# Latent attention of a decoder layer: the next head's projections moved behind this head's scores, its squares behind the exponential

## The reference

```python
q = split_heads(rms_norm(c_q, mla_cq_norm) @ mla_w_uq, MLA_HEADS)       # 256 -> 96 per head
kv = split_heads(rms_norm(c_kv, mla_ckv_norm) @ mla_w_ukv, MLA_HEADS)   # 128 -> 64 + 64 per head
k_nope, v = jnp.split(kv, [MLA_NOPE_DIM], axis=-1)
k = jnp.concatenate([k_nope, k_rope_h], axis=-1)                        # k_rope_h: shared, 32
q, k = rms_norm(q, mla_q_norm), rms_norm(k, mla_k_norm)                 # over the 96
# rope on the last 32 of q and k, then causal softmax attention, scale 96 ** -0.5
o_mla = merge_heads(block_causal_attention(q, k, v)) @ w_branch_mla
g_fox, g_mla = jnp.split(jax.nn.sigmoid(gate_logit + b_gate), 2, axis=-1)
```

## Time and profile before

| | |
|---|---|
| median of 3 runs | 2617.26 us (2610.24 to 2620.54) |
| the profiled execution | 2618.03 us |
| its span | 2616.2 us |
| TensorE busy | 2435.0 us (93%) |
| VectorE busy | 1423.7 us (54%) |
| ScalarE busy | 967.5 us (37%) |
| GpSimd busy | 507.2 us (19%) |
| latent attention | about 1190 to 1757 us from the span's start |

### The profile page before, as it was taken

How to read it: one execution, slowest core, us unless ns; L and a number is a source line. 1 busy time by engine, 2 the same in 40 slices (tenths; PEclk the granted TensorE clock), 3 DMA queues, 4 the chain that set the end, 5 groups by cost and what they waited for, 6 DMA issues and landing times. The chain is left out here.

```text
span 2616.2 us, 37156 instructions
## 1 busy us (share of the span) xinstructions
PE 2435.0 (93%) x14204; PEld 2155.9 (82%) x14204; DVE 1423.7 (54%) x2052; ACT 967.5 (37%) x1619; POOL 507.2 (19%) x634
## 2 busy tenths in 40 slices
PE   6999999999959999977998999989998999999999
PEld 6899999999958887876777777778876888887887
DVE  7665555555456557533444444445367666555553
ACT  5332333333245444432333333335234333333332
POOL 0023200000033244321222222232320323000000
PEclk8999999999979999989999998889998999999999
DMA  4365632565230000011111110014432676336653
GB/s 182 124 211 188 216 110 100 224 222 182 85 129 1 26 25 1 1 33 43 36 36 34 34 35 28 28 47 151 169 137 82 201 230 216 119 103 242 221 194 112
DMA packets 132699, 298.00 MB, mean 114 GB/s; under 512 B 10096, under 2 KB 57072, under 8 KB 129216
## 3 DMA queue, kind: packets, MB, share of 16 engines
q1 hardware_dynamic: 132544, 295.88, 32.7%
HBM read 206.99 MB, written 88.72 MB: 113 GB/s over the span
## 5 line engine op out<-in xcount | busy, mean ns | idle before, releaser
L1070 DVE TENSOR_TENSOR f_w_lo<-f_rw,f_w_hi 128x1024 fp32r<-128x1024 f32 x154 | 196.2, 1274 | 221.4 <-ACT f_w_hi L590 221.4
L833 PE MATMUL f_ps<-u_hi,f_w_hi 128*128 128x260 f32 (+1 forms) x1056 | 284.0, 323 | 25.9 <-DVE f_w_lo L1070 13.2
L833 PE MATMUL f_ps<-u_lo,f_w_hi 128*128 128x260 f32 (+1 forms) x1056 | 283.0, 323 | 0.0
L833 PE MATMUL f_ps<-u_hi,f_w_lo 128*128 128x260 f32 (+1 forms) x1056 | 282.6, 322 | 0.0
L590 ACT CAST f_w_hi<-f_rw 128x1024 fp32r<-128x1024 f32 x154 | 161.2, 1047 | 164.6 <-PE f_ps L833 157.4
L833 PE MATMUL f_ps<-f_far_hi,f_w_hi 128*128 128x260 f32 (+1 forms) x792 | 211.9, 322 | 8.7 <-DVE f_ev L1086 8.7
L833 PEld LDWEIGHTS f_ps<-u_hi,f_w_hi 128*128 128x128 f32 x1056 | 178.3, 192 | 42.3 <-DVE f_w_lo L1070 14.6
L833 PE MATMUL f_ps<-f_far_lo,f_w_hi 128*128 128x260 f32 (+1 forms) x792 | 210.9, 321 | 0.0
L833 PE MATMUL f_ps<-f_far_hi,f_w_lo 128*128 128x260 f32 (+1 forms) x792 | 210.7, 320 | 0.0
L833 PEld LDWEIGHTS f_ps<-u_hi,f_w_lo 128*128 128x128 f32 x1056 | 177.9, 192 | 14.2
L833 PEld LDWEIGHTS f_ps<-u_lo,f_w_hi 128*128 128x128 f32 x1056 | 177.7, 191 | 14.2
(11 more groups left out here) (394 smaller groups left out, 6128.5 us busy)
## 6 DMA issues: line engine op xcount, KB each, us to landing
f_rw<-in_gu SPq DMA_DIRECT2D x88, 512.0 KB, 4.4
f_rw<-kept_dsum SPq DMA_DIRECT2D x32, 704.0 KB, 5.1
f_rw<-kept_hid SPq DMA_DIRECT2D x33, 520.0 KB, 5.6
f_rw<-in_down SPq DMA_DIRECT2D x24, 704.0 KB, 4.2
f_rw<-kept_hid SPq DMA_DIRECT2D x33, 512.0 KB, 5.5
h_in<-in_wd SPq DMA_DIRECT2D x11, 1024.0 KB, 7.0
kept_dsum<-h_in SPq DMA_DIRECT2D x44, 256.0 KB, 3.0
h_out<-in_wd SPq DMA_DIRECT2D x11, 1024.0 KB, 7.3
```

Source lines behind the costliest of these rows:

```text
L833: last = nc.tensor.matmul(out[:, b, 0:N], w[:, c], u[:, b * N:(b + 1) * N], start=(j < 3 and k == 0 and i == 0), stop=(k == 3 and i == 2), ...
L1070: nc.vector.tensor_tensor(slot(w_lo, st), src, slot(w_hi, st).bitcast(F32), ALU.subtract).then_inc(wlo_done, 1)
```

## The change

It changes the order on two engines. On TensorE, `products` of the next head moves from the head of the block to the place behind `scores`; in the first head's own preparation it moves behind the first maxima and gates of the block. On ScalarE, the square is taken out of `early` and made a function of its own, which is called behind `exponential` (and, in the first head's preparation, behind `copy_logits`).

```diff
@@ ScalarE: early, square @@
                     nc.scalar.copy(split_of(h, u)[0][0:DK, t0:t0 + n], x32[0:DK, u % 2, 0:n]).then_inc(xhi_done, 1)
+
+            def square(p, h, w):
                 if w < NU:
                     is_q, c = units[w]
                     t0, n = QK_TOKENS[c]
@@ ScalarE: head @@
                     exponential(p, h, w)
                     if more:
+                        square(p, h + 1, w)
                         late(p, h + 1, w)
                         gate_weights(p, h + 1, w, more=next_gate)
@@ ScalarE: first head's preparation @@
             for w in range(NW):
                 early(0, 0, w)
                 copy_logits(0, 0, w)
+                square(0, 0, w)
                 late(0, 0, w)
                 gate_weights(0, 0, w)
@@ TensorE: head @@
                 for w in range(NW):
-                    if more and w < NU:
-                        products(p, h + 1, w)
                     if more:
                         maxima(p, h + 1, w, 0)
                         gates(p, h + 1, w, 0)
                     scores(p, h, w)
+                    if more and w < NU:
+                        products(p, h + 1, w)
                     if more:
                         maxima(p, h + 1, w, 1)
                         gates(p, h + 1, w, 1)
@@ TensorE: first head's preparation @@
             for w in range(NW):
+                maxima(0, 0, w, 0)
+                gates(0, 0, w, 0)
                 if w < NU:
                     products(0, 0, w)
-                maxima(0, 0, w, 0)
-                gates(0, 0, w, 0)
                 maxima(0, 0, w, 1)
                 gates(0, 0, w, 1)
                 prepare(0, 0, w)
```

## The result

The change makes the kernel faster: 2556.43 us (median of 4 runs, 2553.94 to 2561.75) against 2617.18 us (4 runs, 2610.24 to 2620.54), a ratio of 0.9774 with a 95% interval of 0.9749 to 0.9799. The forecast was 2559. The profiled execution took 2556.62 us, its span is 2554.8.

The account below looks back on a forecast made before the run. TensorE was taken as the bound, losing time to projection waits and the lower clock; 33.8 - 1.4 - 0.7 + 27 = 58.7 us, and 2618.0 - 58.7 - 0.8 = 2559 us, range 2543 to 2588.

Parts of the forecast that it names:

- Projections: In blocks 2 to 5 of seven heads, gates and scores cover the scaling: waits 47.8 to 14 us, 33.8 back.
- Squares: In block 0 of seven heads, the sums wait 0.1 us for the later square: +0.7 us.
- Row of maxima: In block 0, the last score product waits 0.2 us for the DMA, seven times: +1.4 us.
- First head's preparation: Before the seven heads, gains and costs of the new order sum to 0, between -3 and +3 us.
- Clock: In the seven heads, low-level running behind the projection waits mostly goes: 27 us back, bounds 0 and 34.
- The rival that the dips stay: Sparse sums, broadcasts and small scores cause the low clock; 31.7 us come back, 2586 us; chance 0.17.
- The ring: Exponential, square, sums, inverse root, GpSimd's iteration and remainder form a loop lengthening all 42 blocks: 2634 us; chance 0.02.
- the wait for the squares: TensorE's wait moves to the sums, half a microsecond each; 21 of 31.7 us go, 2607 us; chance 0.03.
- a wait that slips along: VectorE's scaling slips by as much as the projection, so it waits as before: 2617 us; chance 0.03.

Follow-up runs that it names:

- b: The changed kernel with the projections back at the head of the block, squares still behind the exponential: 2629.34 us, ratio to before 1.0046.
- c: The changed kernel with the projections behind one gate group but ahead of the scores: 2570.46 us, ratio 0.9824.
- h: The changed kernel with d's edit, and the finish of the head before one block earlier (FINISH_1 2 to 1): 2545.98 us, ratio 0.9737.
- f: The changed kernel with the first head's preparation in its old order: 2554.81 us in one execution.
- g2: The changed kernel with long TensorE waits, for GpSimd's remainder of the same block, added in blocks 7 to 12: 2686.63 us in one execution.
- g3: The changed kernel with one wait a head, for GpSimd's remainder of the same block, in block 10: 2570.77 us in one execution.
- g1: The changed kernel with short TensorE waits, for the exponential of the same block, added in blocks 7 to 12: 2592.22 us in one execution.
- a: The changed kernel with the square back ahead of the logit copy and the exponential in the seven heads: 2566.36 us, ratio 0.9802.
- d: The changed kernel with the k scaling reading the bank first and k projections waiting only for that: 2547.80 us, ratio 0.9756.

## Why the prediction was right

**The bound and the place.** TensorE was the bound, and the projections' waits were the loss: b brings them back and with them the whole time. Of the 60.7 us by which the seven heads shortened the sum gave 58.7. The forecast for the total, 2559, is 2.6 us above the median. That it comes so near is in part luck: what lies outside the seven heads adds up to 0.7 us between the two profiled spans (5.8 - 1.6 - 4.9), and of its parts only the preparation's place was in the sum. The 4.9 in particular is the dip in the last head of the traced execution of before.

**Projections.** Predicted: 14 us of waits stay, 33.8 come back. Measured at the weight loads: 15.3 stay, 32.5 come back. In TensorE's own idle time 42.5 us (25.2 + 17.3) have become 8.9, so 33.6 come back:
```profile
PE mla_bank L2438 <- DVE mla_x L2627: 7.7, 14, 0.8
PE mla_bank L2435 <- DVE mla_x L2614: 1.2, 7, 0.2
```
The forecast by block was 0.21, 0.85, 0.33 and 0.58 us; the timeline shows 0.24, 0.85, 0.25 and 0.83 at the loads. Two of them, from one head of the kernel after (block 3's with what follows it):
```profile
1321.17 0.94 PEld L2435 LDWEIGHTS mla_bank<-cq,mla_w_head 128*128 128x128 f32 x4 [0.24 <-DVE mla_x L2614]
...
1326.70 0.59 ACT L2385 ACTIVATE mla_rden<-mla_bank 64x512 f32<-64x512 f32 x1
...
1327.33 0.63 ACT L2387 ACTIVATE mla_rden<-mla_rden 64x512 f32<-64x512 f32 x1
...
1327.97 0.19 PEld L2438 LDWEIGHTS mla_bank<-ckv,mla_w_head 128*64 128x64 f32 x2 [0.85 <-DVE mla_x L2627]
...
1328.39 0.59 ACT L2373 COPY mla_logit<-mla_bank 128x512 f32<-128x512 f32 x1
1329.02 0.19 PEld L73 LDWEIGHTS mla_bank<-u_hi,mla_gate_hi 128*128 128x128 f32 x1 [0.86 <-ACT mla_logit L2373]
```
Block 5, whose scores I priced at 0.70 without a row of their own, is off at the loads alone: TensorE's idle time there is 0.40 us, which is the 1.80 of before less the cover of 1.41, and in block 3 it is 0.70 against 1.80 - 1.14 = 0.66. The cover counts by its length, the gate group's (c) and the scores'.

**The copy of the logits** was the term left out. Its row grew by 4.1 us, but most of that passes while the projection still streams: in block 3 the next gate product starts 0.96 to 1.08 us behind the start of the k projection in six of the seven heads, against 0.79 in the seventh, before and in h, and that adds up to 1.5 us. The same rows show where it comes from: in block 3 ScalarE finishes the head before (lines 2385 and 2387) from 1326.70 to 1327.96, then makes x_hi, and only then copies the logits; TensorE, which used to spend that time waiting for the scaling, now comes to the next gate product sooner, and its load waits 0.86 us there (the product, at 1329.02, has 0.20 us of idle TensorE before it). The prediction named this copy in the first head's preparation and not in the seven heads. What was late next should have been asked of ScalarE too; h confirms the place.

**Squares**: 0.7 us predicted, 0.3 measured. **Row of maxima**: 1.4 predicted, 2.1 measured (7 waits, 0.4 at most). **First head's preparation**: 0 predicted within 3, -1.6 measured, and by f -1.8. Block 0 of the same head, for the first two of these:
```profile
1311.74 0.19 PEld L2530 LDWEIGHTS mla_bank<-mla_q_hi,mla_k_hi 98*128 98x128 f32 x1 [0.23 <-DMA mla_q_hi<-mla_m_lo]
1312.08 1.45 PE L2435 MATMUL mla_bank<-cq,mla_w_head 128*128 128x384 f32 x4
...
1313.57 0.49 ACT L2334 ACTIVATE mla_sq<-mla_bank 96x384 f32<-96x384 f32 x1 [0.70 <-PE mla_bank L2435]
1314.36 0.77 PE L2461 MATMUL mla_bank<-ones,mla_sq 96*128 96x1 f32 x6
```
The last score product waits 0.23 us for the rows (0.2 was worked out), and the square ends 2.0 us after the projection's start, 0.3 before the sums begin.

**Clock.** I took 27 of 34 us; all of the 64.8 low microseconds went, and TensorE was busy in 63.8 of them, which is 63.8 / 2 = 31.9 us. The terms of the sum then read: 33.6 + 31.9 - 1.5 - 2.1 - 0.3 = 61.6, 0.9 more than the 60.7; the row of maxima and the squares are taken from the loads, and so at their upper bound. With the rows of the loads throughout it would be 32.5 + 32.4 - 4.1 - 2.1 - 0.3 = 58.4. TensorE's "issue" waits of line 73, which fell from 16.2 to 9.6 us, are in neither.

What did not hold is the reason given for this term: that a wait lowers the clock only behind a broadcast and a row of one-column sums. g2 and g3 show the low level behind waits between dense products. What counts there is first the length of TensorE's idle time. In g2, 26 of the 28 idle times of 1.6 to 2.7 us were followed by a low stretch, and 3 of the 14 of 1.0 to 1.4; in g3, four of seven of 1.7. Before the change, 16 low stretches stood behind the 28 waits: behind 10 of the 14 with 1.8 to 1.9 us of idle TensorE and behind 6 of the 14 with 1.2 to 1.3. With at most 1.2 (c) or 0.8 us (g1 and the change) there is none in the seven heads. The idle time need not be one piece: in a, in one head of seven, the low stretch follows an idle 1.04 us that came behind another of 0.70, 1.9 us from the end of one to the end of the other.

But the part about the neighbours isn't refuted whole. Idle times of 1.22 us behind broadcast and sums were followed by the low level in 5 of 12 cases before the change, and those of 1.07 to 1.19 us behind a gate group in none of 14 in c. No run has the same length in both places, so what the gate group does beside shortening the wait stays open. The change does both, and its waits are well below either; so the price came out right though the reason isn't whole.

The rival that the dips stay, 17 in 100, fell: none is left in the seven heads. The Trainium skill (TensorE: Matmul & The Clock Gate, "Why this matters for your kernels") warns only of idle gaps longer than the 1.7 us of g3; here the trace disagrees, since shorter ones lower the clock too, and the measurement decides. The ring, the wait for the squares and a wait that slips along did not show: the scaling does hang on the broadcast alone, 2.7 us before a k projection in every order of the queue (c).

## What to carry to other kernels

Price a moved instruction by the work that then lies between it and what it waits for, block by block; that came out within 1.3 us of 47.8 at the weight loads and within 0.2 in TensorE's idle time. Read what a wait costs from the bound engine's products, not from its loads. Then ask the same of every other engine that the bound engine meets in those blocks, since it arrives sooner everywhere: the copy of the logits took back 1.5 us here, and d shows 4.0 of 7.2 us going to it again until its own engine was freed. Waits in which TensorE is idle for 1.2 us or more can be worth more than their length here, because the products behind them may run at the lower level; how often they do is in the counts above.

## What had not been expected of the hardware

- A single wait of 1.7 us between rows of dense products was followed by 3.4 us at a granted clock of 0.51 in four of seven heads (g3), and in a two idle times of 0.70 and 1.04 us close together had the same effect in one head of seven. In the last head two of 0.7 us, 3 us apart, stand ahead of 13.7 us at the lower level in 4 of 14 traces. The same code can fall to the lower level in one execution and not in another.
- A gate group of three products of 512 columns, 0.71 us long, shortened the wait of the weight load behind it by only 0.45 us (c), but TensorE's idle time by 0.71. A row of waits of weight loads is no measure of the time lost: 4.1 us more of them cost 1.5 (the copy of the logits).
- The phases ahead of latent attention, the same in all kernels, ended between 1188.2 and 1199.5 us in the profiled executions: more than the difference between several of these kernels, which is why the seven heads and not the totals were compared.
